# Hybrid decoder step on one core: the recurrence's outputs laid out with tokens on partitions, squares and scales on ScalarE, gates applied directly

## The reference, cut to what matters

```
h  = rms_norm(x, norm1)
u, q, f, i, g = split(h @ w_in)                 # 1024 columns each
pool part      = pool_mix(u)                    # trailing means, a small map, a scale
forget = lb + (1 - lb) * sigmoid(f);  k = 1 - forget;  q = silu(q)
per head (8 heads, 128 x 128 state):  S_t = diag(forget_t) S_{t-1} + k_t^T i_t;   o_t = q_t S_t
o = o * rsqrt(mean(o*o over the head's 128) + 1e-6) * hg_norm * silu(g)
x = x + concat(pool part, o) @ w_o
x = x + (silu(h2 @ w_gate) * (h2 @ w_up)) @ w_down,   h2 = rms_norm(x, norm2)
outputs: rms_norm(x), and the new pooling rows and states
```

## Time and profile before

| | us |
|---|---|
| median of 3 runs (lowest, highest) | 1520.35 (1520.12, 1521.35) |
| the profiled execution's own time | 1519.69 |
| its span | 1517.9 |
| TensorE busy in the span | 1463.0 |
| VectorE, ScalarE, GpSimd busy | 792.6, 560.7, 239.3 |
| mean granted TensorE clock | 0.981 of full speed |

### The profile page before, as it was taken

The page is one execution under the profiler, slowest core; times in us unless marked ns, Lnnn a source line. Parts: engine busy times, 40 slices in busy tenths (PEclk is TensorE's granted clock), DMA queues, the critical chain, the costliest instruction groups (busy, mean ns, idle before and its releaser), DMA issues.

```text
span 1517.9 us, 26905 instructions
## 1 busy us (share of the span) xinstructions
PE 1463.0 (96%) x9816; PEld 1441.3 (95%) x9816; DVE 792.6 (52%) x1214; ACT 560.7 (37%) x831; POOL 239.3 (16%) x410
## 2 busy tenths in 40 slices
PE   7998989889989999999999999999999999999996
PEld 5998988889979999999999999999999999999996
DVE  4556776666755555544444444444444444544443
ACT  6443434434333334333333333333333333333343
POOL 0265345454502220000000000000000000000131
PEclk9999999998989999999999999999999999999998
DMA  8554434445435555554555554556555456555453
GB/s 228 143 133 127 115 97 126 118 134 139 114 100 136 141 152 149 141 154 132 141 162 158 151 153 130 145 149 168 154 139 156 128 145 177 141 155 149 114 142 118
DMA packets 409519, 214.58 MB, mean 141 GB/s; under 512 B 4093, under 2 KB 407757, under 8 KB 409420
## 3 DMA queue, kind: packets, MB, share of 16 engines
q1 hardware_dynamic: 391207, 203.59, 49.2%
q10 hardware_dynamic: 18277, 10.52, 2.4%
HBM read 206.20 MB, written 7.89 MB: 141 GB/s over the span
## 4 chain that ended last, share of the span: by engine, by line
PE 83%; DVE 6%; POOL 4%; issue 3%; ACT 2%; DMA 1%; ACTq 0%; DVEq 0%; POOLq 0%; SPq 0%
PE bank L383 26%; PE bank L384 26%; PE bank L385 26%; POOL km L1555 2%; DVE qr L1224 1%; POOL kp L1564 1%; DVE w_lo L1039 1%; ACT w_hi L695 1%; PE bank L523 1%; DVE sc L1239 1%; DMA xt<-in_x_sample 1%; PE bank L551 0%; PE bank L479 0%; DVE sn L1283 0%; DVE t L1211 0%
## 5 line engine op out<-in xcount | busy, mean ns | idle before, releaser
L383 PE MATMUL bank<-a_hi,w_hi 128*128 128x320 f32 x2048 | 645.4, 315 | 0.0
L384 PE MATMUL bank<-a_lo,w_hi 128*128 128x320 f32 x2048 | 638.9, 312 | 0.0
L385 PE MATMUL bank<-a_hi,w_lo 128*128 128x320 f32 x2048 | 638.7, 312 | 0.0
L1039 DVE TENSOR_TENSOR w_lo<-w_raw,w_hi 128x1024 fp32r<-128x1024 f32 (+1 forms) x416 | 460.0, 1146 | 161.3 <-ACT w_hi L695 159.9
L695 ACT ACTIVATE w_hi<-w_raw 128x1024 fp32r<-128x1024 f32 (+1 forms) x416 | 387.2, 967 | 164.7 <-PE bank L385 137.9
L383 PEld LDWEIGHTS bank<-a_hi,w_hi 128*128 128x128 f32 x2048 | 390.2, 191 | 2.5
L384 PEld LDWEIGHTS bank<-a_lo,w_hi 128*128 128x128 f32 x2048 | 390.4, 191 | 0.8
L385 PEld LDWEIGHTS bank<-a_hi,w_lo 128*128 128x128 f32 x2048 | 390.0, 190 | 0.0
L383 PE MATMUL bank<-h_hi,w_hi 128*128 128x320 f32 x704 | 217.7, 309 | 0.0
L384 PE MATMUL bank<-h_lo,w_hi 128*128 128x320 f32 x704 | 216.5, 308 | 0.0
L385 PE MATMUL bank<-h_hi,w_lo 128*128 128x320 f32 x704 | 216.5, 308 | 0.0
(11 more groups left out here) (228 smaller groups left out, 1245.3 us busy)
## 6 DMA issues: line engine op xcount, KB each, us to landing
w_raw<-in_w_gate SPq DMA_DIRECT2D x44, 1024.0 KB, 5.6
w_raw<-in_w_up SPq DMA_DIRECT2D x44, 1024.0 KB, 5.6
w_raw<-in_w_down SPq DMA_DIRECT2D x64, 704.0 KB, 4.8
w_raw<-in_w_in SPq DMA_DIRECT2D x39, 1024.0 KB, 5.8
w_raw<-in_w_o SPq DMA_DIRECT2D x16, 1024.0 KB, 6.0
s<-in_state_hgrn ACTq DMA_DIRECT2D x8, 512.0 KB, 6.6
out<-sn ACTq DMA_DIRECT2D x8, 512.0 KB, 6.5
xt<-in_x_prompt SPq DMA_DIRECT2D x3, 512.0 KB, 9.2
```

The source lines that it names most:

```text
L383: pe.matmul(out, whi[:, par_, cols], r_hi, start=(k == 0), stop=False)
L384: pe.matmul(out, whi[:, par_, cols], r_lo, start=False, stop=False)
L385: last = pe.matmul(out, wlo[:, par_, cols], r_hi, start=False, stop=(k == last_k))
L1039: dve.tensor_tensor(wlo[:, par_, cols], raw[:, par_, cols], whi[:, par_, cols].bitcast(F32), SUB)\
```

## The change

The outputs of a head are computed with tokens on partitions (three blocks of 128, 128 and 64 rows), by exchanging the two operands of each product. ScalarE squares each block with a running sum per row (`oss`), takes the root of the mean, and later scales each row (`rec_scale`); three transposes turn the result back into `OT` (`rec_back`). The sample states' products now have 32 masked query columns (`qm`) as the stationary operand and 128 moving columns. `Tanh` of f/2 replaces the sigmoid in `forget` (with altered constants), `Silu` replaces sigmoid times value for q and for the gate. GpSimd's `query` and `gate` go. Heads 0 to 4 have units f, q, v, g in this order, so that the gate is ready when the head's output is turned back, and one VectorE instruction (`rec_gate`) applies norm weight and gate; heads 5 to 7 have three units each and the three gate units at the end; the outputs of heads 5 and 6 are kept in `onb`.

```diff
-W2 = H0 + 6
-W7 = W2 + 4 * EARLY
-G0 = W7 + 3
+L0 = H0 + 4 * EARLY
+G0 = L0 + 3 * (HEADS - EARLY)
...
@@ TensorE @@
 rec_scores: matmuls on zq in place of qq; the wait on ostd before the value transposes goes
             def rec_s0(r):
                 pe.wait_ge(s0_loaded, 16 * (r + 1))
-                after(pe, on_ready, r)
-                for b in range(NB):
-                    t = slice(TP + b * TS, TP + (b + 1) * TS)
-                    pe.matmul(OT[:, t], s0[:, b, :], qr[LS][:, t], start=(b == 0), stop=False)
+                pe.wait_ge(qm_ready, r + 1)
+                out = OT[:, TP:TP + P]
+                for i in range(HB):
+                    for j in range(2):
+                        b = HB * j + i
+                        at = QSTEP * b - TS * i
+                        pe.matmul(out[j * HS:(j + 1) * HS, :], qm[:, at:at + HS], s0[:, b, :], start=(i == 0), stop=False)
             def rec_out(r):
-                rec_s0(r)
+                if isinstance(r, int) and r > EARLY:
+                    pe.wait_ge(o_kept, r - EARLY)
+                else:
+                    after(pe, gated, r)
                 pe.wait_ge(s1_ready, r + 1)
                 pe.wait_ge(sc_put, PUTS * (r + 1))
-                pe.matmul(OT[:, 0:CH], vt[:, 0, :], sc[:, 0, :], start=False, stop=False)
...
+                pe.matmul(OT[:, 0:P], sc[:, 0, :], vt[:, 0, :], start=True, stop=True)
+                pe.matmul(OT[:, P:TP], sc[:, 1, :], vt[:, 1, :], start=True, stop=False)
+                pe.matmul(OT[:, P:TP], qr[LP][:, CH:TP], s1[:, :], start=False, stop=True)
+                rec_s0(r)
+                pe.matmul(OT[0:NS, TP:TP + P], scs[:, :], vt[0:NS, 2, :], start=False, stop=True).then_inc(o_mm, 1)
...
-            def rec_stat(r):
-                pe.wait_ge(o_read, 2 * (r + 1))
-                token_stats(TV, (osq,), 1, ostat_mm)
-            def rec_bcast(r):
-                pe.wait_ge(odiag, r + 1)
-                to_all(OT, obc_mm)
+            def rec_back(r):
+                pe.wait_ge(o_scaled, r + 1)
+                pe.transpose(OT[:, 0:P], tm[:, 0, :], ident)
+                pe.transpose(OT[:, P:TP], tm[:, 1, :], ident)
+                pe.transpose(OT[:, TP:N], tm[0:NS, 2, :], ident[0:NS, 0:NS]).then_inc(o_back, 1)
+            scored(H0 + 3, 1, 0)                       # scores and state of head 0
+            with pe.Fori(0, EARLY - 1) as i:
+                put_out(H0 + 4 * i + 4, 0, i)          # rec_out in the middle
+                turned_back(H0 + 4 * i + 5, 1, i)      # rec_back at the end
+                unit(H0 + 4 * i + 6, 0, a_rhs)
+                scored(H0 + 4 * i + 7, 1, i + 1)
...
+            for r in range(EARLY, HEADS - 1):
+                n = L0 + 3 * (r - EARLY) + 3
+                scored(n, n % 2, r)
+                put_out(n + 1, (n + 1) % 2, r)
+                turned_back(n + 2, n % 2, r)
+            scored(G0, 1, HEADS - 1)
+            put_out(G0 + 1, 0, HEADS - 1)
+            unit(G0 + 2, 1, a_rhs, after_tile=last_back)   # rec_back after block 12; before: rec_bcast after block 8
@@ ScalarE @@
             def forget(h, n):
-                act.activation(sgm[:, :], zf[:, :], ACT.Sigmoid).then_inc(zf_sig, 1)
+                act.activation(zf[:, :], zf[:, :], ACT.Tanh, scale=0.5).then_inc(zf_tanh, 1)
...
+            def silu_q(h, n):
+                act.wait_ge(unit_read, n + 1)
+                act.activation(zq[:, :], zq[:, :], ACT.Silu).then_inc(q_ready, 1)
+            def silu_g(g, n):
+                act.wait_ge(unit_read, n + 1)
+                after(act, gm_lo, g)
+                act.activation(ga[:, :], zf[:, :], ACT.Silu).then_inc(g_act, 1)
             def rec_squares(r):
                 act.wait_ge(o_mm, r + 1)
-                act.activation(osq[:, :], OT[:, 0:N], ACT.Square).then_inc(o_read, 1)
-                act.activation(osb[:, :], OT[:, 0:N], ACT.Copy).then_inc(o_read, 1)
+                after(act, o_back, r)
+                for i in range(3):
+                    rows = P if i < 2 else NS
+                    last = act.activation(tm[0:rows, i, :], OT[0:rows, i * P:(i + 1) * P], ACT.Square,
+                                          accum_out=oss[0:rows, i:i + 1])
+                last.then_inc(o_squared, 1)
+                act.wait_ge(o_squared, r + 1)
+                act.activation(stat[:, 6:9], oss[:, :], ACT.Identity, bias=epst[:, 0:1], scale=1.0 / P)
+                act.activation(stat[:, 0:3], oss[:, :], ACT.Sqrt, bias=epst[:, 0:1], scale=1.0 / P).then_inc(o_std, 1)
+                act.activation(warm[:, 0:1], epst[:, 0:1], ACT.Silu)
+            def rec_scale(r):
+                act.wait_ge(newton_step, 4 * (r + 2))
+                for i in range(3): ...                 # tm[rows, i] = OT block * stat[rows, 3 + i]; then o_scaled
+            def turn(n, h, r):
+                split_hi(n + 1, 1);  silu_g(r, n - 1);  rec_squares(r);  load_s0(h);  rec_stores(r)
+                forget(h, n);  split_hi(n + 2, 0);  rec_scale(r);  silu_q(h, n + 1);  split_hi(n + 3, 1)
+                gate_split(r);  split_hi(n + 4, 0)      # then rec_tokens of the next head
+            def short_turn(n, h, r):
+                split_hi(n + 1);  rec_tokens(r);  forget(h, n);  split_hi(n + 2);  rec_squares(r);  load_s0(h)
+                rec_stores(r);  silu_q(h, n + 1);  split_hi(n + 3);  rec_scale(r)
@@ VectorE @@
 queries: reads zq in place of qq; one more product into qm, and level 2 shortened to 256 columns
-            rec_rms (with diagonals), rec_norm, rec_lo, gate_apply, gate_product
+            rec_newton (no diagonals)
+            def rec_gate(r, src):
+                dve.wait_ge(g_act, r + 1)
+                dve.scalar_tensor_tensor(out=ga[:, :], in0=src, scalar=pcol("hg_norm", r), in1=ga[:, :],
+                                         op0=MUL, op1=MUL).then_inc(gated, 1)
+            first_part:   split_lo(n + 1);  rec_sample_state(r);  scaled(n) -> zf
+            second_part:  split_lo(n + 1);  products(h);  rec_newton(r);  scaled(n) -> zq
+            third_part:   split_lo(n + 1);  rec_gate(r, OT);  queries(h);  gate_lo(r);  values(n)
+            scores_part:  split_lo(n + 1);  rec_scores(r);  rec_sample_lo(r);  scaled(n) -> zf;  rec_state(r)
+            short heads:  scores_part;  split_lo;  rec_sample_state;  products;  scaled -> zq;  split_lo
+                          rec_newton;  queries;  values
@@ GpSimd @@
-            query, gate
+            per head: keys(h), key_copies(h), rec_sample(h);  qm is zeroed with sc and scs
```

More of the change, by code:

```diff
@@ L333, in _ @@
                     load(2 * i + k, k, win_v, (0, KD), (2 * i + k) * P)
-            for h in range(2):
+            with sp.Fori(0, EARLY) as h:
+                for j, part in enumerate((2, 1, 3, 4)):
+                    load(H0 + 4 * h + j, j % 2, win_v, (0, KD), part * PW + h * P)
+            for h in range(EARLY, HEADS):
                 for j, part in enumerate((2, 1, 3)):
[L336 to L342, removed]
+                    n = L0 + 3 * (h - EARLY) + j
+                    load(n, n % 2, win_v, (0, KD), part * PW + h * P)
             for g in range(EARLY, HEADS):
-                load(G0 + g - EARLY, 1 - (g - EARLY) % 2, win_v, (0, KD), 4 * PW + g * P)
+                n = G0 + g - EARLY
+                load(n, n % 2, win_v, (0, KD), 4 * PW + g * P)
             with sp.Fori(0, KD // 2) as i:
@@ L1326, in values, with first_part, second_part, third_part @@
                 turned(n, par_).then_inc(unit_read, 1)
-            def window(n, par_, h, r):
+            def first_part(n, par_, r):
+                split_lo(n + 1, 1 - par_)
+                rec_sample_state(r)
+                dve.wait_ge(g_act, r + 1)
+                scaled(n, par_, zf[:, :]).then_inc(unit_read, 1)
+            def second_part(n, par_, h, r):
+                split_lo(n + 1, 1 - par_)
+                products(h)
+                rec_newton(r)
+                scaled(n, par_, zq[:, :]).then_inc(unit_read, 1)
+            def third_part(n, par_, h, r):
+                split_lo(n + 1, 1 - par_)
+                dve.wait_ge(o_back, r + 1)
+                rec_gate(r, OT[:, 0:N])
+                queries(h)
+                gate_lo(r)
+                values(n, par_)
+            def scores_part(n, par_, r):
                 split_lo(n + 1, 1 - par_)
@@ L1388, in _ @@
-            rec_state(HEADS - 1)
+            scores_part(H0 + 3, 1, 0)
+            with dve.Fori(0, EARLY - 1) as i:
+                first_part(H0 + 4 * i + 4, 0, i)
+                second_part(H0 + 4 * i + 5, 1, i + 1, i)
+                third_part(H0 + 4 * i + 6, 0, i + 1, i)
+                scores_part(H0 + 4 * i + 7, 1, i + 1)
+            first_part(L0, 0, EARLY - 1)
+            second_part(L0 + 1, 1, EARLY, EARLY - 1)
+            third_part(L0 + 2, 0, EARLY, EARLY - 1)
+            for r in range(EARLY, HEADS - 1):
+                n = L0 + 3 * (r - EARLY) + 3
+                a = n % 2
```

(20 more changed lines are left out.)

305 lines of the change are left out of this document (117 added, 188 removed).

## The result

| | before | after |
|---|---|---|
| median, us (lowest, highest) | 1520.23 (1515.75, 1521.35) | 1480.94 (1478.37, 1481.55) |
| profiled execution; its span | 1519.69; 1517.9 | 1481.55; 1479.6 |
| TensorE busy; mean clock | 1463.0; 0.981 | 1436.7; 0.987 |

The ratio is 0.9744, 95% interval 0.9721 to 0.9766.

What follows compares the result with a forecast made beforehand. A chain through ScalarE, VectorE and GpSimd, not TensorE's work, was taken to bound the rounds. Gains of 14 (long rounds), 6.6 (short), 4.8 (head 7) and 0.5 (head 0), together 25.9, taken as 25, gave 1495 us, range 1487 to 1508.

Steps and rivals of the forecast that it cites:

- F to the back transposes: From the end of the unit making the output (F) to its transposes back: 9.96 us kept, pause growing to 2.9.
- Table loads: On ScalarE: two loads per round instead of four, each costing 1.28 us and nothing behind it.
- the s copy: Copy before the output products: 10.3 us after first score product, no wait; rival, 5%: it stays late, kernel slower, 1532.
- S to F: From a head's first score product (S) to the end of its output unit (F): 18.9 us, bounds 18.0 and 20.9.
- Outputs: Sample products on TensorE with operands exchanged: 1.8 us, plus 0.1 taken, bounds 0.8 and 4.3.
- F to S: From output unit's end (F) to the next head's first score product (S): 22.5 us instead of 24.5, bounds 21.5 and 24.0.
- the short round: Round of three units between heads' scores: 31.8 us against 35.1, two of them gaining 6.6.
- head 7: From the last head's scores to the first w_o unit: 30.6 us against 35.4, gaining 4.8.
- head 0: Before the first scores: queries now wait for the masks' clearing, but low parts come first; gain 0.5 us.
- Late queries: Rival, 14%: VectorE stays late at the queries, so only TensorE's own work goes; 1508 us.
- tables: Rival, 8%: Tanh and Silu need different tables, two more loads per round on the path; 1503 us.
- The clock holds: Rival, 7%: shorter pauses leave TensorE's clock up, up to 1.5 us more per long round; 1487 us.

Runs made afterwards that it cites:

- e3: Kernel after the change, with the finished query passed once more through GpSimd behind the keys and VectorE waiting for it: 1497.4 us, ratio 0.9853.
- e4: Kernel before the change, with only the query altered: one Silu on ScalarE, GpSimd's query multiplication gone: 1493.33 us, ratio 0.9827.
- e7: Kernel after the change, with Sigmoid instead of Tanh in the forget gate, so two more table loads per round: 1485.68 us, ratio 0.9776.
- e2: Kernel after the change, with the sample products run column group by column group instead of alternating: 1483.99 us, ratio 0.9765.
- e10: Kernel after the change, with the masked query columns cleared by VectorE itself instead of GpSimd: 1473.33 us, ratio 0.9695.
- e9: Kernel after the change, with twelve unused float32 matmuls before the back transposes of heads 0 to 4, filling the pause: 1474.12 us, ratio 0.9695.
- e1: Kernel after the change, with VectorE taking the Newton step before the low parts and the products: 1479.17 us, ratio 0.9727.
- e5: Kernel after the change, with each head's first key copies moved from GpSimd to ScalarE: 1479.57 us, ratio 0.9744.
- e6: Kernel after the change, with both the early Newton step and the first key copies on ScalarE: 1468.73 us, ratio 0.9684.

## Why the prediction was wrong in size

**Right.** The direction and the mechanism: the chain through GpSimd's `qq` bound all rounds, and its removal is worth 16.5 (put back in the kernel after, e3) to 26.9 (taken from the kernel before, e4) of the 39.3. *F to the back transposes* was forecast 9.96 and is 10.0, with a pause of 2.84 for 2.9. *Table loads*: two a round, none before Tanh or Silu, no drain (e7). No wait for the s copy, which ends at S+8.7 where 10.3 was forecast. From the transposes to S it is 13.2 us in the round shown, 1.53 of it low clock; 11.7 without, and 11.5 was forecast (12.5 with the lower clock).

**Failed: S to F, 18.9 us with a lower bound of 18.0; it is 16.92** in seven of the eight heads (19.4 in head 0, with lower clock behind its wait). *Outputs* failed in "I take plus 0.1": the sample records got 0.8 us shorter (1.07 for 1.85 occupied) and the whole block 0.81 (2.68 for 3.49). I had the possibility as the lower bound, 0.8, and did not use it: L558's spacing, which I took, is that of matmuls with 128 stationary columns. Of the 0.81, 0.46 is the alternation (e2); the remaining 0.35 was not taken apart. The other 1.2 of the 2.0 missed is the 0.1 added there and some 1.1 of lower clock and of a slower start of the scores that I kept in the term. In five heads the lower clock stands behind the wait before the scores, which my own text removed. But in three (S at 251.70, 339.40 and 384.65, the second of them one of the five) it sets in at the end of the output block, with no idle before it. TensorE of before behind the block of the third:

```profile
398.91 0.31 PE L383 MATMUL bank<-a_hi,w_hi 128*128 128x320 f32 x1
...
399.27 0.47 PE L385 MATMUL bank<-a_hi,w_lo 128*128 128x320 f32 x1
399.53 0.47 PE L383 MATMUL bank<-a_hi,w_hi 128*128 128x320 f32 x1
```

e4, which took the score waits away and kept the block, shows the same in three heads (from 212.12, 253.15 and 294.46 on); no trace of a kernel with the new block shows it. So these 1.5 us in each of three heads left with the block, and I had not seen them. Which property of the block brings them was not tested. Over the five long rounds S to F gives 7.4 us more than forecast and F to S, 23.1 on average for 22.5, takes 2.9 back: that is the 4.5 between 207.0 (five times 41.4) and 202.5.

**Failed: the short round, 31.8; it is 28.53.** I had VectorE's list end at S+30.3. It ends at S+26.8 (358.0 for S at 331.21), 3.5 sooner: 2.0 sooner because S to F is shorter, and the queries take 4.0 with `qm` instead of the 5.8 I kept "as now" and 0.2 for `qm`; other items of the list take 0.5 of this back. The row of 4.97 was a duration with GpSimd's product beside it (e3), and the change moved that product away; in e4, with the old 320 columns, the queries take 4.2. With VectorE early, TensorE is the bound, and my own sum of TensorE's work, 30.4, less 2.0 for S to F is the 28.5 measured. Two such rounds are 6.5 of the 12.8 us by which the terms (25.9) fell short of 38.7.

**Failed: head 7, 30.6; it is 27.99.** The scaled rows were forecast at S+26.9; the back transposes start at S+25.0 (413.23), after 2.17 us of idle. That is S to F again.

**Failed: head 0, a gain of 0.5; it is a loss of 0.5** and a low clock after it. I wrote that the low parts come first; the masks' clearing stands behind GpSimd's key chain, and VectorE waited 6.4 us for it (e10).

**The rivals.** Late queries, tables and the s copy did not happen. *The clock holds* was priced at up to 1.5 us per long round; it held in two of five, and 1.28 on average is still lost (e9). The range was too narrow because each term's bounds were taken from rows of before, in which the wait that the change removed was still at work, and because the 18.0 for S to F left out the prediction's own lower bound for the sample products (with it, 17.95 less 0.9 is 17.05).

## What to carry to other kernels

When a wait is taken away, every duration read next to it is open again: the clock behind the wait comes up, and an engine that ran beside another no longer does. Look, before moving one chain, for the second one that ends in the same pause; two edits worth nothing alone that could be told gave 9 to 12 us together (e1, e5, e6), and where a pause can't be closed, harmless matmuls in it can be worth more than their time (e9).

## What the runs showed of the hardware

- Sixteen records with 32 stationary and 128 moving columns take 1.07 us when two column groups alternate and 1.53 when they follow each other.
- VectorE's steps with two SBUF inputs lost 1.9 us beside one GpSimd product of 2.15 us (e3). In the kernel of after, a pair of GpSimd's key products (128x64) takes 0.55 us while VectorE stands still (119.08), 1.41 at 282.38 and 2.48 at 114.92, beside VectorE's low parts.
- Idle of 2.84 to 2.86 us was followed by matmuls at 0.267 us spacing in three of four cases of one execution (after) and in two of four of another (e10), idle of 2.60 in neither, and idle of 3.4 to 3.7 us in all five cases of e7. Idle of 4.0 us at head 0 was followed by them too, and 2.84 us filled with matmuls never in five cases (e9).
- The same spacing set in with no idle at all behind the old output block in three of eight heads, in before and in e4, for 1.5 us each.
- Tanh and Silu follow each other with no table load; a load takes 1.28 us, and ScalarE's next instruction starts at its end (after and e7).
